# A decoder step's kernel: sample attention moved directly behind the prompt, one joint merge of the other 448 tokens, and another order of the gathers

## What is computed

```python
def dsa_sample(...):      # sparse attention of the 64 new tokens: an indexer scores all 2056 keys
    scores = where(admissible, index_scores(q_i, w_i, k_idx_all), NEG)
    vals, sel = top_k(scores, 256)              # attention over the 256 chosen keys
def fox_sample(...):      # forgetting attention of the same tokens over all 2056 keys
    s_past = einsum(q, kp) * ATTN_SCALE + tail + cn
    p = softmax(concatenate([s_past, s_new]))
def finish_layer(...):
    merged = sigmoid(g_a) * (y_a @ w_branch_a) + sigmoid(g_b) * (y_b @ w_branch_b)
    h = layer_norm(ALPHA * x + merged @ w_out)
    f = peer(h)           # per token: 8 heads x top 16 of 128*128 experts,
                          # sum_k gate_k * gelu(u_k . h) * v_k
    return layer_norm(ALPHA * h + f)
```

## Time and profile before

| | |
|---|---|
| median of 3 runs | 2402.66 us (2399.91 to 2403.54) |
| span of the profiled execution | 2493.9 us (no other time of it is shown) |
| busy share PE, DVE, ACT, POOL | 73%, 57%, 12%, 52% |
| mean granted clock of TensorE | 0.853 of full speed |
| HBM read | 784.13 MB |

### The profile page before, as it was taken

How to read it: one execution, slowest core, us unless ns; L and a number is a source line. 1 busy time by engine, 2 the same in 40 slices (tenths; PEclk the granted TensorE clock), 3 DMA queues, 4 the chain that set the end, 5 groups by cost and what they waited for, 6 DMA issues and landing times.

```text
span 2493.9 us, 23573 instructions
## 1 busy us (share of the span) xinstructions
PE 1810.2 (73%) x7244; PEld 768.0 (31%) x7247; DVE 1433.9 (57%) x3191; ACT 307.8 (12%) x732; POOL 1307.8 (52%) x1175
## 2 busy tenths in 40 slices
PE   9999988899699635566666766776777884555566
PEld 6767646644244201111112121221223250110011
DVE  2115876898845643999856569854444437434400
ACT  0214442111011101001101010110110010000000
POOL 1100000467655744555555557766777747677664
PEclk9998987999899867777778789998999997876678
DMA  5206322999989976999999999999999999999997
GB/s 182 71 3 195 102 85 68 355 328 410 361 306 368 346 281 238 394 367 400 386 401 380 401 371 362 371 356 368 378 384 409 409 370 374 364 359 380 355 377 287
DMA packets 259648, 791.92 MB, mean 318 GB/s; under 512 B 31522, under 2 KB 56163, under 8 KB 258947
## 3 DMA queue, kind: packets, MB, share of 16 engines
q0 software_dynamic: 166400, 604.58, 63.6%
q1 hardware_dynamic: 91268, 180.82, 20.6%
q10 hardware_dynamic: 1856, 5.03, 0.5%
HBM read 784.13 MB, written 5.59 MB: 317 GB/s over the span
## 4 chain that ended last, share of the span: by engine, by line
POOL 13%; DMA 10%; PE 8%; issue 7%; SPq 7%; another core or an unknown queue 6%; DVE 2%; ACT 1%; POOLq 0%
POOL arena L918 13%; DMA arena<-v_b 4%; PE ps L1369 3%; SPq L841 3%; DMA arena<-peer_v,arena 3%; SPq L768 2%; DMA arena<-peer_u,arena 2%; PE ps L1325 2%; DMA arena<-kv_a 2%; SPq L834 1%; PE ps L1202 1%; DVE arena L2081 1%; PE ps L1302 1%; ACT arena L1640 0%
## 5 line engine op out<-in xcount | busy, mean ns | idle before, releaser
L1369 PE MATMUL ps<-arena 128*32 128x512 f32 x2304 | 767.5, 717 | 346.6 <-DMA arena<-peer_v,arena 287.9
L2081 DVE CUSTOM_DVE_ANT_0 arena<-arena 128x1024 f32<-128x1024 f32 x576 | 694.7, 1225 | 531.5 <-DMA arena<-peer_u,arena 475.7
L918 POOL DMA_INDIRECT arena<-peer_v,arena x576 | 623.4, 1082 | 445.9 <-PE ps L1369 245.0
L918 POOL DMA_INDIRECT arena<-peer_u,arena x576 | 664.1, 1153 | 311.8 <-issue 162.2
L1369 PEld LDWEIGHTS ps<-arena 128*32 128x32 f32 x2304 | 153.4, 122 | 877.7 <-issue 662.1
L1164 PE MATMUL ps<-arena 128*128 128x448 f32 (+2 forms) x512 | 156.8, 467 | 13.1 <-DVE arena L1997 12.4
L1202 PE MATMUL ps<-arena 128*128 128x384 f32 (+2 forms) x704 | 146.5, 368 | 10.0 <-ACT arena L1576 8.1
L1325 PE MATMUL ps<-arena 128*64 128x512 f32 (+1 forms) x512 | 102.6, 538 | 68.1 <-DMA arena<-v_b 57.3
L900 POOL MEMSET arena<- 128x1024 f32 x1 | 1.0, 953 | 282.4 <-ACTq L723 282.4
L950 PE MATMUL ps<-arena 128*128 128x296 f32 (+1 forms) x512 | 132.1, 419 | 6.2 <-DMA arena<-xT 6.2
L1699 ACT ACTIVATE arena<-arena 128x8 f32<-128x8 f32 x72 | 15.3, 216 | 943.1 <-PE ps L1369 635.2
(11 more groups left out here) (211 smaller groups left out, 1694.1 us busy)
## 6 DMA issues: line engine op xcount, KB each, us to landing
arena<-k_b SPq DMA_DIRECT2D x128, 256.0 KB
arena<-v_b SPq DMA_DIRECT2D x128, 256.0 KB
arena<-w_mix SPq DMA_DIRECT2D x56, 512.0 KB
arena<-w_q SPq DMA_DIRECT2D x48, 512.0 KB
arena<-kv_a SPq DMA_DIRECT2D x128, 128.0 KB
arena<-w_out SPq DMA_DIRECT2D x24, 512.0 KB
arena<-peer_u,arena POOLq DMA_INDIRECT x576
arena<-peer_v,arena POOLq DMA_INDIRECT x576
```

The lines of the kernel that those rows point to most:

```text
L918: pool.indirect_dma_start(out=rows[slot_of[n]], out_offset=None, in_=io["peer_v"] if v else io["peer_u"], in_offset=bass.IndirectOffsetOnA ...
L1369: last = pe.matmul(bank(6 + a, 512, 32 * lane, 32 * lane + 32), strips[:, GT * (G % 2) + k % GT, MID - r_:MID - r_ + 32], rows[slot_of[n]] ...
L2081: dve.tensor_tensor_reduce(out=row, in0=row, in1=h, scale=1.0, scalar=0.0, op0=ALU.mult, op1=ALU.add, accum_out=pre[:, k:k + 1]).then_inc( ...
```

## The change

- **Order of gathers.** u of tile 0, all 128 v of tile 0 (128 to 255), all 128 u of tile 1 (256 to 383), then u of tiles 2, 3 woven with v of tiles 1, 2 one to one, u of tile 4 (64) with 64 v of tile 3, the other 64 v of tile 3, v of tile 4.
- **Sample attention** starts at gather 4 and its items have gaps of 1 in place of 2 to 36: it lies over gathers 4 to 159. SP loads `kidx` right after tile 0's query weights and the first four mix weights.
- **One merge** for tiles 1 to 4 (448 tokens) behind it, from gather 161: branch and query products get 448 columns, tile 4 has output products of its own with a second read of `w_out` (`out_product(2, k)`, in the banks of tile 1), the other weights of merge 2 and the second copy of `ln` go. Its gaps are shorter: `score` 1,0 is at 238, `score` 3,3 at 269, `score` 4,3 at 282.
- **Routing.** Tile 1's sixteen steps lie at 240 to 272, tile 2's at 279 to 354, the others 110 gathers ahead of their u rows as before. `SWITCH` is 310 in place of 790.
- **Memory.** The sample results go into `yaT`, `ybT`; the ring of cache pages, `osb` and `relu_s` move to `hrow`, `ln` and `sc`, so `subk` and these are loaded again behind the sample attention; `hrow[4]` has a place of its own.

```diff
-        later = vs[1] + vs[2] + vs[3]
-        ALONE = 72
-        gathers = us[0] + vs[0][:ALONE] + weave(us[1], vs[0][ALONE:]) + weave(us[2], later[:120]) + weave(us[3], later[120:244]) + later[244:320]
-        gathers += weave(us[4], later[320:370]) + later[370:] + vs[4]
+        gathers = us[0] + vs[0] + us[1] + weave(us[2], vs[1]) + weave(us[3], vs[2]) + weave(us[4], vs[3][:64])
+        gathers += vs[3][64:] + vs[4]
...
-                size = 4 if span == 3 else 2 if gather_at[i, 1, k] > gather_at[4, 0, 0] - 130 else 1
+                size = 4 if span == 3 else 2
...
             if p:
-                out += [(("mix", p, 0), (0, 10, 6)[p])]
+                out += [(("mix", 1, 0), 5)]
                 for m in range(1, KD):
-                    out += [(("mix", p, m), (0, 3, 1)[p]), (("mixed", p, m - 1), (0, 7, 3)[p])]
-                out += [(("mixed", p, KD - 1), 1)]
-                out += [(("out", p, k), (0, 4, 2)[p]) for k in range(KD)]
-                out += [(("norm", i), 1 if p == 1 else 4) for i in tiles]
-            out += [(("turn", i), 2 if i == 3 else 1) for i in tiles]
+                    out += [(("mix", 1, m), 2), (("mixed", 1, m - 1), 3)]
+                out += [(("mixed", 1, KD - 1), 1)]
+                out += [(("out", 1, k), 2) for k in range(KD)]
+                out += [(("norm", i), 1) for i in (1, 2, 3)]
+                out += [(("out", 2, k), 0) for k in range(KD)] + [(("norm", 4), 1)]
+            out += [(("turn", i), 1) for i in PASS[p]]
             for m in range(2 * PH):
-                out.append((("query", p, m), (2, 4, 1)[p]))
+                out.append((("query", p, m), (2, 2)[p]))
...
         def sample_items():
-            out = [(("zero",), 0), (("spread", 0), 1), (("ix", 0), 3), (("iy", 0), 34), (("ix", 1), 12)]
+            out = [(("zero",), 0), (("spread", 0), 1), (("ix", 0), 1), (("iy", 0), 6), (("ix", 1), 4)]
             for c in range(2, 5):
-                out += [(("ix", c), 2), (("iy", c - 1), 14 if c == 2 else 3)]
+                out += [(("ix", c), 1), (("iy", c - 1), 6 if c < 4 else 1)]
...
-                        out += [(("s_score", q + 1, c), 5), (("s_weigh", q, c), 5)]
+                        out += [(("s_score", q + 1, c), 1), (("s_weigh", q, c), 1)]
...
-        at = 0
-        for item, gap in merge_items(1):
-            put(at, *item)
-            at += gap
...
-        at = s_start = m1_end + 2
+        at = 4
         q_at_ = {}
         for item, gap in sample_items():
...
-        top_from, top_to = q_at_[("admit",)] + 2, q_at_[("s_out", 3)] + 24
+        top_from, top_to = q_at_[("admit",)] + 1, q_at_[("s_out", 3)] + 1
...
-        at = s_end + 4
-        for item, gap in merge_items(2):
+        at = s_end + 2
+        for item, gap in merge_items(1):
             put(at, *item)
             at += gap
...
+        for g in range(4):
+            at = max(at, where["score", 1, g] + 2)
+            for s_ in range(4):
+                put(at, "route", 1, g, s_)
+                at += 2
...
+        SWITCH = -(-(where["score", 4, 3] + 24) // NR0) * NR0
         for i in (2, 3, 4):
             u0 = gather_at[i, 0, 0]
-            at = u0 - 110
+            at = max(u0 - 110, where["gate", 1] + 2)
...
+        merge_weights = [("mix", 0, m, part) for m in range(KD) for part in range(2)]
+        merge_weights += [("mix", 0, m, 2) for m in range(KD)]
+        merge_weights += [("out", 0, k, 0) for k in range(KD)] + [("query", 0, m, 0) for m in range(2 * PH)]
+        merge_weights += [("mix", 1, m, part) for m in range(KD) for part in range(3)]
+        merge_weights += [("out", p, k, 0) for p in (1, 2) for k in range(KD)] + [("query", 1, m, 0) for m in range(2 * PH)]
...
+            def first_queries():
                 sp.dma_start(subk[:], io["subk"]).then_inc(subk_loaded, 16)
-                for w in range(first_query + 2 * NMW, first_of_last):
+                for w in range(first_query + 2 * NMW, first_mix + NMW):
                     weights(w)
...
+            def second_merge():
+                sp.wait_ge(se_ready, NB)
+                for i in range(1, 5):
+                    if i == 4:
+                        sp.wait_ge(se_done, NB)
+                    x_rows(i)
+                sp.dma_start(lng, io["ln"][0:1, :].partition_broadcast(128)).then_inc(ln_loaded, 16)
+                sp.dma_start(lnb, io["ln"][1:2, :].partition_broadcast(128)).then_inc(ln_loaded, 16)
+                sp.dma_start(subk[:], io["subk"]).then_inc(subk_loaded, 16)
+                for w in range(first_mix + NMW, len(merge_weights)):
+                    weights(w)
...
                 for c in range(4):
-                    if c:
-                        sp.wait_ge(sc_ready, 13 + c)
-                    else:
-                        sp.wait_ge(mix_done, KD)
+                    if c == 3:
+                        sp.wait_ge(sc_ready, 4)
...
-            first_merges()
+            first_queries()
             sample()
-            last_merge()
+            second_merge()
             pack_last()
...
                 if k == 0:
-                    pe.wait_ge(mix_done, KD * p)
-                    if p == 1:
-                        turned_before("out", p, k)
+                    pe.wait_ge(mix_done, KD)
+                    turned_before("out", p, k)
+                    if p == 2:
+                        pe.wait_ge(res_done, 2)
```

More of the change, by code:

```diff
@@ L192, in program @@
         ya_at = base.at
[L193 removed]
+        yaT, ybT = base.take(4, SEQ + NS), base.take(4, SEQ + NS)
         a_end = base.at
@@ L289, in program @@
         b_at = r.at
-        hT_all = r.take(KD, 384)
+        hT_all = r.take(KD, REST)
         subk = r.take(2 * PH, 128)
-        sig = [r.take(384) for _ in range(2)]
+        sig = [r.take(REST) for _ in range(2)]
         assert r.at <= b_end, (r.at, b_end)
@@ L518, in sample_items @@
             for c in range(2, 5):
-                out += [(("ix", c), 2), (("iy", c - 1), 14 if c == 2 else 3)]
-            out += [(("iy", 4), 2), (("admit",), 1)]
-            out += [(("s_score", 0, c), 5) for c in range(5)]
-            out += [(("s_max", 0), 2), (("s_exp", 0), 2), (("s_norm", 0), 2), (("s_turn", 0), 3)]
+                out += [(("ix", c), 1), (("iy", c - 1), 6 if c < 4 else 1)]
+            out += [(("iy", 4), 1), (("admit",), 1)]
+            out += [(("s_score", 0, c), 1) for c in range(5)]
@@ L523, in sample_items @@
+            out += [(("s_max", 0), 1), (("s_exp", 0), 1), (("s_norm", 0), 1), (("s_turn", 0), 1)]
             for q in range(NB):
@@ L547, in program @@
         put(42, "gate", 0)
-        at = 0
-        for item, gap in merge_items(1):
-            put(at, *item)
-            at += gap
-        m1_end = at
-        for g in range(4):
-            for s_ in range(4):
-                put(where["score", 1, g] + 2 + 3 * s_, "route", 1, g, s_)
-        put(where["route", 1, 3, 3] + 2, "gate_in", 1)
-        put(where["route", 1, 3, 3] + 5, "gate", 1)
-        at = s_start = m1_end + 2
+        at = 4
         q_at_ = {}
@@ L569, in program @@
         put(top_to, "mask")
-        at = s_end + 4
-        for item, gap in merge_items(2):
+        at = s_end + 2
+        for item, gap in merge_items(1):
             put(at, *item)
             at += gap
-        m4_end = at
-        SWITCH = -(-(s_end + 24) // NR0) * NR0
+        m1_end = at
+        at = 0
+        for g in range(4):
[3 more added lines that the diff above has]
+                at += 2
+        put(where["route", 1, 3, 3] + 2, "gate_in", 1)
+        put(where["route", 1, 3, 3] + 5, "gate", 1)
+        for g in range(4):
+            put(where["gate", 1] + 2 + g, "score", 4, g)
+        SWITCH = -(-(where["score", 4, 3] + 24) // NR0) * NR0
         for i in (2, 3, 4):
             u0 = gather_at[i, 0, 0]
-            at = u0 - 110
-            assert i < 4 or at > m4_end, (at, m4_end)
+            at = max(u0 - 110, where["gate", 1] + 2)
             for s_ in range(16):
@@ L583, in program @@
             put(at + 88, "gate", i)
+        assert where["score", 4, 3] > where["gate", 1]
         for i in range(5):
@@ L590, in program @@
                 put(max(n + (3 if last else 14), 47 if i == 0 else 0), "coefs", i, g)
-        bank4 = [(where["mix", p, m], where["mixed", p, m]) for p in (1, 2) for m in range(KD)]
+        bank4 = [(where["mix", 1, m], where["mixed", 1, m]) for m in range(KD)]
         bank4 += [(where["s_score", q, 4], where["s_exp", q]) for q in range(NB)]
@@ L1161, in mix @@
                         pe.wait_ge(mix_done, n)
-                    out = bank(2 * (n % 2) + j, GATES1) if j < 2 else bank(2 + j, w)
+                    out = bank(2 * (n % 2) + j if j < 2 else 2 + j, w)
                     for k in range(nk):
@@ L1710, in _ @@
             for kind, *at in plan:
-                if kind == "mix" and at[0] == 1:
+                if kind == "mix":
                     sigmoids(*at)
```

149 lines of the change are left out of this document (59 added, 90 removed).

## The result

The changed kernel took 2787.26 us (median of 4 runs, 2781.33 to 2796.49), the kernel before 2401.28 us (4 runs, 2398.26 to 2403.54): a ratio of 1.161, 95% interval 1.157 to 1.165. It is 386 us slower. The forecast was 2700 us, its range 2590 to 2850.

A forecast was written before the change was run, and what follows sets the result against it. Transfers bound the kernel before. From 429 us the changed kernel's stages were summed to `admit` at 636, then 946, 1094, 1427, 1682, 2783 and the end at 2803; times 0.9634 that is 2700 us, range 2590 to 2850.

The forecast's parts named there:

- the rival on the other side: Behind the prompt, transfers stay the limit, making the kernel faster: 2321 us; gather 256 asked for before 1118 us; chance 0.05.
- A: From 429 us to `admit`: 128 uncovered key-load issues on SP, taken as 165 us; `admit` at 636.
- B: Four forgetting pairs, gathers 34 to 94: fills plus softmax waits, 310 us, ending at 946.
- C: Four sparse pairs, gathers 95 to 160: SP's loads at about 37 us per pair, 148 us, ending at 1094.
- D: Joint merge until gather 256 can be asked for: PE is the limit, 333 us (300 to 350), ending at 1427.
- E: Tile 1's key rows alone, gathers 256 to 383: VectorE reads and routing, 255 us (240 to 275), ending at 1682.
- F, G: Last 768 gathers at 1.434 us, 1101 us (1075 to 1115), plus 20 us after the last issue; end at 2803.
- the hole of the earlier trace: Start of the kernel before's sample attention, 835 to 981 us: DMA at 0.78 while SP issues 128 key loads.
- The ring-bound rival: Forgetting pairs keep today's loading pace with its waits, 430 us; whole kernel 2816 us; chance 0.12.
- The landmark: Asking for gather 256, behind which both kernels have the same 896 gathers; about 903 us in the kernel before.
- The factor 0.9634: Scaling of the whole sum from profiled to run time, 2402.66 / 2493.9: 2803 becomes 2700 us.

The follow-up runs named there:

- experiment 2: Changed kernel with the indexer keys loaded by 32 fixed loads of 128 KB instead of 128 of 32 KB: 2703.05 us, ratio to before 1.125.
- experiment 3: Kernel before with the indexer keys loaded by 32 fixed loads of 128 KB instead of 128 of 32 KB: 2398.05 beside 2400.87 us, ratio 0.998.
- experiment 1: Kernel before, unchanged, profiled once more: the profiled execution took 2392.3 us with a span of 2390.3.
- experiment 4: Changed kernel with the sparse pairs' key and value pages loaded by 16 fixed loads of 1 MB instead of 128 of 128 KB: 2759.17 us.
- experiment 5: Changed kernel with the joint merge's gate products over 4 of their 8 chunks, all weights still loaded: 2743.0 us.
- experiment 7: Kernel before with the new order of gathers alone: 2433.41 beside 2400.83 us, ratio 1.012.
- experiment 6: Changed kernel with routing of tiles 2 and 3 placed pair of heads by pair, just ahead of their key rows: 2780.73 us, ratio to before 1.158.
- experiment 8: Kernel before with the short gaps of the sample attention alone, second merge starting 60 gathers behind: 2588.77 us, ratio 1.078.
- the added compares: Changed kernel with two unread VectorE compares of 384 elements per partition behind each of 70 reads of tile 3's key rows: 2787.55 us.
- copies: Changed kernel with four unread VectorE copies of 384 elements per partition behind each of 70 reads of tile 3's key rows: 2785.40 us.
- sums: Changed kernel with two unread VectorE sums of 384 elements per partition behind each of 70 reads of tile 3's key rows: 2793.37 us.

## Why the prediction was right, and where it was off

The mechanism was right: gather 256 is asked for at 1464.2 us where the sum had 1427, far behind the 1118 us from which the rival on the other side would have decided. By its steps, in span time, forecast and measured:

| step | forecast | measured | |
|---|---|---|---|
| A, to `admit` | 207 | 193 | 128 issues took 145.6 us; the low bound 146, not the 165 taken |
| B, forgetting pairs | 310 | 309 | |
| C, sparse pairs | 148 | 209 | the term that failed |
| D, merge to gather 256 | 333 | 324 | mix 146.5 (146), outputs 42.3 + 15.9 (57) |
| E, key rows alone, gathers 256 to 383 | 255 | 260 | VectorE 241 of 260 |
| F, G | 1121 | 1059 | 768 gathers at 1.346 us, not 1.434; 25 behind the last, not 20 |
| span | 2803 | 2783.7 | |

PE's groups of D, for its terms:

```profile
L1152 PE MATMUL ps<-arena 128*128 128x448 f32 x384 | 146.5, 540 | 0.0
L1195 PE MATMUL ps<-arena 128*128 128x448 f32 x183 | 70.9, 542 | 0.7 <-ACT arena L1560 0.7
...
L1167 PE MATMUL ps<-arena 128*128 128x512 f32 x96 | 42.3, 596 | 0.0
L1167 PE MATMUL ps<-arena 128*64 128x512 f32 x32 | 15.9, 655 | 2.1 <-DMA arena<-w_out 2.1
```

**A** was right in kind: experiment 2 puts 84 us on its issues, experiment 3 none in the kernel before. Its evidence, the hole of the earlier trace rows, was not a property of the kernel (experiment 1), and with it falls what the prediction held against the rival on the other side at this point, the 0.78 at 835 to 981. The pace of the earlier trace rows, 1.14 us per load, was the kernel's: 145.6 us for 128 is the same. The 0.95 us that the Trainium skill gives ("DMA: Bandwidth & Descriptors", Measured), for a load issued from GpSimd's queue and not from SP's, would have been 122 us, an estimate. That these loads leave the engines empty holds only where little else is in flight, as in the changed kernel once the 43 gathers are out (columns as above):

```profile
520.00:606.00 86.00, 13.44 (x20) 4.93 (x20) 7.76 (x18) 2.88 (x5) 5.32 (x4) 0.58 0.20 60
```

**C** is the step that failed. The prediction took "SP's kv loads take 31.5 to 39.6 us per pair, about 37, four times 148", as if a pair were its loads. It is the loads and then the chain, 28 and 21 us, because four fills are one pair and the ring has four slots (the timelines of experiment 4). For B it had added fills and softmax; for C it compared two figures and took the larger. The ring-bound rival had the mechanism, but at the wrong stage.

**D** was sized to 3% from the form rows, and experiment 5 (39 to 44 us of 49 expected) shows PE as its limit. The 13.7 MB that the joint pass saves lie where transfers aren't the limit, as said; what the narrow query products saved was not measured.

**E** was sized to 5 us, and experiment 7 has its kind alone at 33 us in the kernel before. What the sum did not have is POOL: 61 of its 128 issues there take over 1.15 us, 49 us more in all than at 0.94 each. That less routing in E is worth next to nothing (experiment 6) was not foreseen: routing slows gathers in the later stretches too.

**F, G** was 62 us too long, and that is its rate: 1.434 us per gather had been taken from the slower execution, and the changed kernel needs 1.346, with 409 GB/s where issues miss the reads and 352 to 382 where, beside routing above all, they don't. The landmark itself was misread a little in the same profile: gather 256 is asked for at 912.5 us there, not 903.

**The factor 0.9634** is the other step that failed. The sum itself, 2803, was 0.7% above the span. The 91 us between profile and runs belonged to that one execution, not to profiling: spans of the second profile of before and of the changed kernel lie 2 us below their own times. The prediction allowed for this with 20 us only. The factor took 103 us off; without it the forecast is 2803, 16 us above the measured time. That this is so near is luck in part: C and E lacked 66 us, and the other steps had 86 too much.

**Not run**: the change's first part alone (sample attention first with the old gaps). Gaps and order alone give 188 + 33 = 221 of the 386 us, if they add, which was not run either. The other 165 lie in the place, the joint merge and what these do to one another; no run parts them. The 84 us of the keys' issues can't be laid to the place alone, since in experiment 8 the DMA share falls to 0.71 beside the same issues.

## What to carry to other kernels

A stage whose loads are hidden has a price that shows only when its cover goes: before moving it, count its issues and its chain of waits per ring's worth of loads, and ask what else keeps the DMA engines fed at the new place. Where one pass of work fills every slot of a ring, as here, loading and computing follow one another, and their times add (28 and 21 us). And profile the kernel before twice when its profiled time is off its runs: one slow execution gave a wrong hole, a wrong rate and a wrong factor.

## What the runs showed of the hardware that had not been expected

- POOL's issue of a gather of 128 rows of 4 KB takes 0.94 us; one that starts well inside a key-row read of VectorE ends some 0.81 us after the read and so takes up to 1.99 us. All 217 issues over 1.15 us of the changed kernel start in a VectorE instruction with two inputs in SBUF; none of those beside an idle VectorE, a search or a sum does.
- So the rate of these gathers depends on how issues and reads fall: 409 GB/s (1.26 to 1.28 us per gather) where they miss one another, 352 to 382 in the other stretches with rows of value and key woven, 370 beside the added compares, 381 beside copies, 392 beside sums.
- The same 128 issues of 32 KB take 145.6 us with little in flight and 150.3 us beside saturated transfers; 32 issues of 128 KB take 74.0 and 100.6 us. With the small loads the issuing queue sets the pace (DMA share 0.20 from 520 to 606 us), with the larger ones the transfers do (1.06 from 456 to 530 us in experiment 2).
